# A third buffer for the conditioning slabs, single slabs at even distances, and their requests moved within ScalarE's program

## The reference, cut to what matters

```python
# first block
h = h + 0.5 * swiglu(rms_norm(h, ffn1_norm[l]), ffn1_w1[l], ffn1_w3[l], ffn1_w2[l])
...  # attention and pooling
h = h + 0.5 * swiglu(rms_norm(h, ffn2_norm[l]), ffn2_w1[l], ffn2_w3[l], ffn2_w2[l])
# second block, layers 0 and 1
cond = silu(c)
mod = cond @ ada_w[i] + ada_b[i]
sh_m, sc_m, g_m, sh_f, sc_f, g_f = split(mod, 6)
h = rms_norm(x, norm_mix[i]) * (1 + sc_m) + sh_m
```

## Time and profile before

| | us |
|---|---|
| median of 3 runs | 3036.22 |
| lowest, highest | 3034.94, 3041.8 |
| profiled execution, own time | 3037.72 |
| its span, first to last instruction | 3035.9 |
| TensorE busy | 2819.2 (93%) |
| VectorE busy | 1431.1 (47%) |
| GpSimd busy | 868.0 (29%) |
| ScalarE busy | 539.6 (18%) |

### The profile page before, as it was taken

How to read it: one execution, slowest core, us unless ns; L and a number is a source line. 1 busy time by engine, 2 the same in 40 slices (tenths; PEclk the granted TensorE clock), 3 DMA queues, 4 the chain that set the end, 5 groups by cost and what they waited for, 6 DMA issues and landing times.

```text
span 3035.9 us, 28890 instructions
## 1 busy us (share of the span) xinstructions
PE 2819.2 (93%) x11348; PEld 2009.3 (66%) x11348; DVE 1431.1 (47%) x2231; ACT 539.6 (18%) x1019; POOL 868.0 (29%) x688
## 2 busy tenths in 40 slices
PE   7998999999999998999999989999996459999999
PEld 6887885655446787885544755888543224688888
DVE  6444312156525544323279353555415992466531
ACT  2000000011201000001112251222115431222200
POOL 4444430000213433430000132443012560344432
PEclk9999999999999999999599999999997669999999
DMA  6444322211123444321011102224220001222222
GB/s 208 148 158 150 122 76 83 65 62 42 56 69 128 146 159 156 116 77 60 14 56 56 56 1 70 84 97 111 76 66 28 0 1 56 80 86 84 86 78 73
DMA packets 222626, 253.37 MB, mean 83 GB/s; under 512 B 16328, under 2 KB 209180, under 8 KB 222364
## 3 DMA queue, kind: packets, MB, share of 16 engines
q1 hardware_dynamic: 207996, 199.32, 20.8%
q10 hardware_dynamic: 14496, 52.21, 4.7%
HBM read 249.41 MB, written 2.10 MB: 83 GB/s over the span
## 4 chain that ended last, share of the span: by engine, by line
PE 79%; DVE 14%; ACT 2%; issue 2%; DMA 2%; POOL 1%; DVEq 0%; ACTq 0%; SPq 0%; POOLq 0%
PE ps L612 33%; PE ps L668 13%; PE ps L1140 9%; PE ps L498 5%; PE ps L1606 3%; PE ps L2277 3%; DVE phase L2435 2%; DMA phase<-in_ada_w 2%; PE ps L1167 1%; PE ps L1647 1%; PE ps L1659 1%; DVE phase L2420 1%; PE ps L890 1%; PE ps L1275 1%; DVE rs L1856 1%
## 5 line engine op out<-in xcount | busy, mean ns | idle before, releaser
L612 PE MATMUL ps<-hT,ring 128*128 128x256 f32 x2816 | 656.6, 381 | 2.6 <-DVE hT L954 1.0
L612 PEld LDWEIGHTS ps<-hT,ring 128*128 128x128 f32 x2816 | 538.5, 192 | 80.4 <-issue 3.5
L612 PE MATMUL ps<-phase,ring 128*128 128x256 f32 x2112 | 516.1, 389 | 53.1 <-DVE act_t L688 51.9
L612 PEld LDWEIGHTS ps<-phase,ring 128*128 128x128 f32 x2112 | 410.4, 195 | 114.8 <-DVE act_t L688 55.9
L540 POOL TENSOR_TENSOR ring<-ring 128x512 f32<-128x512 f32 (+1 forms) x124 | 160.9, 1297 | 1071.3 <-DMA ring<-in_ffn_w 582.7
L668 PE MATMUL ps<-phase,ring 128*128 128x256 f32 x1848 | 400.6, 379 | 1.0 <-issue 1.0
L668 PEld LDWEIGHTS ps<-phase,ring 128*128 128x128 f32 x1848 | 350.6, 190 | 48.8 <-issue 1.4
L1140 PE MATMUL ps<-hT,ring 128*128 128x512 f32 x512 | 228.0, 599 | 3.1 <-ACT phase L1332 2.6
L1606 PE MATMUL ps<-hT,ring 128*128 128x512 f32 x448 | 197.6, 597 | 0.6 <-ACT hT L1036 0.6
L543 POOL TENSOR_TENSOR ring<-ring 128x512 f32<-128x512 f32 (+1 forms) x124 | 188.7, 1522 | 0.0
L694 DVE TENSOR_TENSOR act_t<-u,ps 128x256 f32<-128x256 f32 x176 | 73.4, 421 | 239.1 <-PE ps L612 238.9
(11 more groups left out here) (331 smaller groups left out, 3082.5 us busy)
## 6 DMA issues: line engine op xcount, KB each, us to landing
ring<-in_ffn_w SPq DMA_DIRECT2D x60, 1024.0 KB, 5.5
phase<-in_ada_w ACTq DMA_DIRECT2D x96, 512.0 KB, 6.1
ring<-in_ffn_w_up SPq DMA_DIRECT2D x44, 1024.0 KB, 5.1
ring<-in_w_in SPq DMA_DIRECT2D x19, 1024.0 KB, 5.3
ring<-in_attn_w_in SPq DMA_DIRECT2D x14, 1024.0 KB, 5.2
ring<-in_ffn_w_down SPq DMA_DIRECT2D x8, 1408.0 KB, 6.1
ring<-in_ssm_w_glu SPq DMA_DIRECT2D x8, 1024.0 KB, 5.5
ring<-in_ffn_w_down SPq DMA_DIRECT2D x8, 1024.0 KB, 5.0
```

Of the source, the lines that this page charges most:

```text
L612: mm = pe.matmul(ps[:, 4 * w + bank_of[name], 0:HALF], left[:, c], right[name](c), start=(opens and c == 0), stop=(c == KC // 2 - 1), skip ...
```

## The change

It has five parts.

1. A third slab buffer, in `sq`. A request for slab n now waits for slab n - 3. The semaphores for landed slabs are three.
2. The table is even: one slab behind steps 3 and 5 of each `w` in every pair, 44 in all. There are no double places.
3. The other four slabs (44 to 47) stand in the first round of the down projection, in VectorE's program: ahead of the step after P6, behind the two updates that follow it, behind the step after P7, and behind the update that follows the step after P5.
4. The requests stand at other places of ScalarE's program. Three stand at the start. Then each stands behind the instruction beside which its predecessor by three is used.
5. The position tables use `acc` and `rs` in place of `sq`, and SyncE's request for the positions waits for one more event, the spread of the norm before.

The core of the diff (the exchange of tile names in the tables is left out):

```diff
-        ada_slab = [phase[:, 22528 + j * D:22528 + (j + 1) * D] for j in range(2)]
+        ada_slab = [phase[:, 22528 + j * D:22528 + (j + 1) * D] for j in range(2)] + [sq[:, :, :].rearrange("p j t -> p (j t)")]
...
                 act.activation(x[:, 0:HALF], ps[:, 0, 0:HALF], ACT.Silu).then_inc(silu_done, 1)
+                ada_load(act, k, SLAB_AT[p, 0, 3] + 3)
                 act.wait_ge(quad, quad_up(k, p, 0, 5))
...
                 if p == 0:
-                    ada_load(act, k, 0)
-                    ada_load(act, k, 1)
+                    for n in range(3):
+                        ada_load(act, k, n)
                     first(p, 1)
                 else:
-                    for n in SLAB_AT[p - 1, 1, 3]:
-                        ada_load(act, k, n + 2)
-                    for n in SLAB_AT[p - 1, 1, 5]:
-                        ada_load(act, k, n + 2)
+                    ada_load(act, k, SLAB_AT[p - 1, 1, 5] + 3)
                 silu(p)
-                for n in SLAB_AT[p, 0, 3]:
-                    if n + 2 < SLABS:
-                        ada_load(act, k, n + 2)
                 if p >= 1:
                     first(p, 1)
-                for n in SLAB_AT[p, 0, 5]:
-                    if n + 2 < SLABS:
-                        ada_load(act, k, n + 2)
+                ada_load(act, k, SLAB_AT[p, 0, 5] + 3)
                 after(p)
+                ada_load(act, k, SLAB_AT[p, 1, 3] + 3)
+            ada_load(act, k, SLAB_AT[NP - 1, 1, 5] + 3)
+            ada_load(act, k, SLAB_AT[NP - 1, 1, 5] + 4)
...
+                def slab(n):
+                    if k < 2 and q == 0:
+                        ada_slab_dve(dve, k, SLABS - 4 + n)
+
                 one, two = 2 * q + 1, 2 * q
+                slab(0)
                 dve.wait_ge(u_copied, COPIES0[k] + FC + q + 1)
                 done("P6")
...
+                slab(1)
                 done("P7")
                 dve.tensor_tensor(c22, u, ps[:, bank + 2, 0:HALF], ALU.add).then_inc(quad, 1)
+                slab(2)
                 done("P5")
...
                 quadrant(two, 1, c22).then_inc(quad, 1)
+                slab(3)
                 done("P2")
...
-            return 2 if step == 5 and w == 1 and p in (2, 4, 6, 8) else int(step == 5)
...
+        SLAB_AT = {(p, w, step): 4 * p + 2 * w + (step == 5) for p, w in UP_STEPS for step in (3, 5)}
...
-            if s >= 2:
-                act.wait_ge(ada_step, SLABS * l + s - 1)
+            if s >= 3:
+                act.wait_ge(ada_step, SLABS * l + s - 2)
...
         def positions_load(sp):
             sp.wait_ge(sum_done, 3)
+            sp.wait_ge(spread_done, 3)
```

More of the change, by code:

```diff
@@ L392, in build @@
         gated = sem("gated")
-        slab_loaded = [sem(f"slab_loaded{i}") for i in range(2)]
+        slab_loaded = [sem(f"slab_loaded{i}") for i in range(3)]
         cond_done = sem("cond_done")
@@ L764, in strassen_silu_dve @@
                         if step in (3, 5):
-                            for n in SLAB_AT[p, w, step]:
-                                ada_slab_dve(dve, k, n)
+                            ada_slab_dve(dve, k, SLAB_AT[p, w, step])
                 x, y, g = quadrants[0], quadrants[1], gT[:, 4 * p * HALF:4 * (p + 1) * HALF]
@@ L1042, in build @@
         SLABS = 6 * KC
-        def slabs_after(p, w, step):
-            if step == 3:
-                return 1
-            return 2 if step == 5 and w == 1 and p in (2, 4, 6, 8) else int(step == 5)
-        SLAB_AT, _slabs = {}, 0
-        for _p in range(NP):
-            for _w in range(2):
-                for _step in (3, 5):
-                    SLAB_AT[_p, _w, _step] = range(_slabs, _slabs + slabs_after(_p, _w, _step))
-                    _slabs += slabs_after(_p, _w, _step)
-        assert _slabs == SLABS
+        UP_STEPS = [(p, w) for p in range(NP) for w in range(2)]
+        SLAB_AT = {(p, w, step): 4 * p + 2 * w + (step == 5) for p, w in UP_STEPS for step in (3, 5)}
         SUM_AT = {}
         for _j in range(5):
-            SUM_AT[min(p for p in range(NP) if SLAB_AT[p - 1 if p else 0, 1, 5][-1] >= KC * _j + KC - 1 and p)] = _j
+            SUM_AT[min(p for p in range(1, NP) if SLAB_AT[p - 1, 1, 5] >= KC * _j + KC - 1)] = _j
         def ada_load(act, l, s):
+            if s >= SLABS:
+                return
             j, c = s // KC, s % KC
-            if s >= 2:
-                act.wait_ge(ada_step, SLABS * l + s - 1)
-            act.dma_start(ada_slab[s % 2], a["ada_w_2"][l, c * P:(c + 1) * P, j * D:(j + 1) * D])\
-                .then_inc(slab_loaded[s % 2], 16)
+            if s >= 3:
+                act.wait_ge(ada_step, SLABS * l + s - 2)
+            act.dma_start(ada_slab[s % 3], a["ada_w_2"][l, c * P:(c + 1) * P, j * D:(j + 1) * D])\
+                .then_inc(slab_loaded[s % 3], 16)
         def ada_slab_dve(dve, l, s):
             j, c = s // KC, s % KC
-            part, slab = ada_acc[j % 2], ada_slab[s % 2]
-            dve.wait_ge(slab_loaded[s % 2], 16 * (SLABS // 2 * l + s // 2 + 1))
+            part, slab = ada_acc[j % 2], ada_slab[s % 3]
+            dve.wait_ge(slab_loaded[s % 3], 16 * (SLABS // 3 * l + s // 3 + 1))
             if c == 0:
@@ L1504, in tables_dve @@
         def tables_dve(dve, p):
-            ang, k = sq[:, 0, :], sq[:, 1, :]
+            ang, k = acc[:, :], rs[:, :]
             if p >= 1:
@@ L1529, in tables_act @@
             act.wait_ge(s_ang, 8)
-            act.activation(C("sin"), sq[:, 0, :], ACT.Sin).then_inc(s_sin, 1)
-            act.activation(sq[:, 1, :], sq[:, 0, :], ACT.Abs).then_inc(s_sin, 1)
+            act.activation(C("sin"), acc[:, :], ACT.Sin).then_inc(s_sin, 1)
+            act.activation(rs[:, :], acc[:, :], ACT.Abs).then_inc(s_sin, 1)
             act.wait_ge(s_sin, 2)
-            act.activation(C("cos"), sq[:, 1, :], ACT.Sin, bias=C("half_pi"), scale=-1.0).then_inc(s_sin, 1)
+            act.activation(C("cos"), rs[:, :], ACT.Sin, bias=C("half_pi"), scale=-1.0).then_inc(s_sin, 1)
         r2 = Region()
@@ L2573, in positions_load @@
             sp.wait_ge(sum_done, 3)
-            sp.dma_start(sq[:, 1, :].bitcast(I32), a["positions_2"].to_broadcast([P, T])).then_inc(s_pos, 16)
+            sp.wait_ge(spread_done, 3)
+            sp.dma_start(rs[:, :].bitcast(I32), a["positions_2"].to_broadcast([P, T])).then_inc(s_pos, 16)
         def late_loads(act):
```

## The result

| us | before | after |
|---|---|---|
| median | 3035.72 (4 runs) | 2962.03 (4 runs) |
| lowest, highest | 3034.94, 3041.8 | 2959.73, 2962.45 |
| profiled execution, own time | 3037.72 | 2959.73 |
| its span | 3035.9 | 2957.9 |

The ratio is 0.9751, with a 95% interval of 0.9735 to 0.9768: faster, by 73.7 us between the medians, where 66 were forecast. The stated range was 2961 to 2983: the median of 2962.0 lies just inside its lower edge, and the ratio applied to the 3036.2 that the prediction started from gives 2960.6, just outside it.

The account below looks back on a forecast made before the run. TensorE, busy 93% of the span, bounds the kernel, so only its standing still or lower clock can be won. Savings of 60.3 + 6 - 0 = 66 us off 3036.2 give 2970 us, range 2961 to 2983.

Parts of the forecast that it names:

- The eight waits: Up projections, behind pairs 2, 4, 6, 8: TensorE's waits behind double slabs go, 44.15 us plus 16.1 of slow stretches, 60.3.
- my ten slow stretches: Lower TensorE clock for 8 to 9 us behind each up-projection wait: 16.1 us for eight, 1.70 and 1.58 behind pair 0.
- The double slab's request: End of pair 2: second slab's request, third in ScalarE's row until 116.9 us, leaves VectorE idle 5.93 and TensorE waiting 5.96.
- The two waits behind pair 0: Up projections: GpSimd's sums slow VectorE's chain; less overlap saves 4.5 + 2.9 = 7.4 us, taken as 6, bounds 0 to 11.0.
- How slot 4 and 5 land: Pair 0: an earlier slab request lets slot 4 land about 1.5 us earlier; the next slot likewise meets slabs spread out.
- The third buffer and the requests: Up projections: three places make 18 us, a slab needs 6.1, so VectorE's 51.3 us of waiting goes to about nothing.
- The four slabs in the down projection: Slabs ahead of the steps after P7 and P5 cost nothing, margins 1.3 and 1.4 us; at most 2 us in all.
- the rule of the Trainium skill: VectorE with two SBUF inputs contends with GpSimd reading SBUF; by it, down-projection slabs could cost 5 us in both stages.
- A: Rival: only the eight waits go, those behind pair 0 stay; 2976 us, up to 2979; chance 0.28.
- B: Rival: the waiting changes place, with half of the eight waits left at some ends of pairs; 3006 us; chance 0.07.
- C: Rival, slower: GpSimd's sums fall on every chain behind pairs 1 to 9, 4.5 us each; 3057 us; chance 0.02.
- D: Rival: no change, TensorE finds another thing to wait for at the same eight places; 3036 us; chance 0.03.

Follow-up runs that it names:

- even table: Kernel before with one slab at each place and four slabs in the down projection, two buffers, requests at old places: 2973.6 us, ratio 0.9792.
- the kernel with the buffer alone: Kernel after with the old table of double slabs, none in the down projection, and old request places, leaving only the third buffer new: 2976.5 us, ratio 0.9800.
- the experiment on the end of a pair: Kernel before with one request per pair moved from behind the next pair's first copy to its own pair's end: 2973.2 us, ratio 0.9786.
- one request moved: Kernel before with pair 0's first request (slab 2) moved ahead of the second activation part: 3030.6 us, ratio 0.9983.
- holding GpSimd back: Kernel with the even table, GpSimd's sums of slot 4 made to wait until VectorE's four sums of pair 0 are done: 2960.6 us, ratio 0.9745.
- fillers: Kernel after with extra VectorE operations behind five pairs of the first up projection: 7 to 21 of them 3002.3 us, 1 to 5 of them 2961.5.
- request back: Kernel after with pair 0's first request behind the start (slab 3) put back behind the second activation part: 2965.8 us, ratio 0.9768.
- the slabs together: Kernel after with slabs 45, 46 and 47 together ahead of the step after P7 in the down projection's first round: 2968.4 us in one run.
- the requests' places alone: Kernel before with requests at the new places only; double slabs, two buffers, none in the down projection: 2960.6 us, ratio 0.9749.

## Why the prediction was right or wrong

*The eight waits*, "sum 60.3 us": measured alone, 61.9 (even table), so right, and short by 1.6, within the noise of the medians. The traces show a shortfall too, in TensorE's busy time. It fell by 286.68 - 275.98 = 10.7 us in the first stage and by 10.9 in the second, 21.6, where my ten slow stretches summed to 19.4: about 0.2 us for each of ten restarts. It is there at the full clock as well: in the kernel with the buffer alone the product behind the 1.61 us wait took 1.83 us from its start to the next one's, where its neighbours take 1.73, and the last one ahead of the wait counts as busy to its own end, 0.16 us more.

*The double slab's request*, "third in a row of three that takes until 116.9 us": misread, without weight in the sum. ScalarE's first request behind the copy is the one for slab 12, the double's second; the third was issued at 116.5, when VectorE had slab 12 in work since 114.91. What held the request was the copy alone, 5.8 us ahead of that slab's start, and the experiment on the end of a pair shows the same.

*The two waits behind pair 0*, "I take 6": this is the step that failed, a term that was mis-sized. Kernel after against the even table alone: 2973.6 - 2962.0 = 11.6 us, against an upper bound stated as 11.0. The medians were taken on different occasions (by the two ratios it is 12.4 us, give or take some 7), but the traces bear it out: the two up projections are 4.6 and 8.8 us longer in the kernel with the table alone, and 2.3 us of that lie in their first 32 records, ahead of any of this. The first stage's part was right (all of 2.79 and its slow stretch, 4.5). In the second stage I let three sums run free and left 2.1 us of wait and the slow stretch. But the position tables' two operations stand in the same chain, and I didn't count them, though I had priced them at 2.2 us beside GpSimd for another pair. Here they are after, with step 2 of pair 1:

```profile
928.10 0.42 DVE L1505 CAST acc<-rs 128x512 f32<-128x512 int32 x1
928.55 0.48 DVE L1507 TENSOR_SCALAR acc<-acc,const 128x512 f32<-128x512 f32 x1
...
929.50 0.42 DVE L688 TENSOR_TENSOR act_t<-u,ps 128x256 f32<-128x256 f32 x1
```

And before:

```profile
968.26 1.48 DVE L1511 CAST sq<-sq 128x512 f32<-128x512 int32 x1
969.78 1.36 DVE L1513 TENSOR_SCALAR sq<-sq,const 128x512 f32<-128x512 f32 x1
...
971.61 0.42 DVE L688 TENSOR_TENSOR act_t<-u,ps 128x256 f32<-128x256 f32 x1
```

0.9 us for 2.8: these 1.9 us are most of the 2.1 that were to be left; the slab in the chain gave another 0.5 (1.38 for 1.91). With the wait its slow stretch went too. The working's own 7.4 would then have been 11; that I took 6 of 7.4 made it worse.

*How slot 4 and 5 land*, "about 1.5 us earlier, and the next slot likewise meets its two slabs spread out": slot 4's first sum started 3.1 us earlier in the execution (48.43, not 51.54). Measured from VectorE's slab, which itself started 1.4 us earlier, it was 51.56 - 48.43 = 3.1 us ahead instead of 53.00 - 51.54 = 1.5, so 1.7 us were won, about the size forecast. The second half of the sentence was the wrong way round: slot 5 must not come early too. Counted from the stage's start, GpSimd's sums of slot 4 began 2.5 and 2.9 us earlier after than before, those of slot 5 at the same time to within 0.2 us. In the second stage slot 5 itself landed some 1.5 us later than before; with one request moved it didn't, its sums stood right behind slot 4's, and 3.92 us of wait were left. Neither the sum nor a rival had named this.

*The third buffer and the requests*, "VectorE's 51.3 us of waiting goes to about nothing": right; the kernel after has no such wait. That the places, the table and the buffer are three cures for the same eight waits I had not said; I gave them to the table.

*The four slabs in the down projection*, nothing: right, 142.50 for 142.47, with the steps behind P7 and P5 here:

```profile
320.53 0.41 DVE L811 TENSOR_TENSOR u<-u,ps 128x256 f32<-128x256 f32 x1
...
322.05 0.41 DVE L817 TENSOR_TENSOR u<-u,ps 128x256 f32<-128x256 f32 x1
```

Counted in the time of the kernel before (36.5 us later at the step after P6) they start at 357.0 and 358.6, where the working had 357.2 and 358.9, and three slabs in one place gave the 1.38 us that the margins say. GpSimd was idle here from 312.5 to 330.7 us, so the rule of the Trainium skill (SBUF — State Buffer, "Who interferes with whom") had nothing to act on. Behind pair 0 the traces agree with it: a sum of VectorE of 0.42 us, with both inputs in SBUF, takes 1.37 to 1.51 beside a sum of GpSimd, and holding GpSimd back gave 0.43 again; steps 1 and 2, with one input in PSUM, kept 0.41 and 0.42 us there (62.88 and 63.42 us, before).

*Rivals.* A (only the eight) was the kernel with the table alone, 2973.6 for 2976. B, C and D didn't occur: no end behind pairs 1 to 9 has a wait.

## What to carry to other kernels

Where an engine waits for a transfer, look first at what stands ahead of the request in its issuer's program: one request per pair, moved ahead of one copy, brought 63.7 us of the 73.7. When two engines hinder each other, a late chain grows (seven fillers of some 0.45 us took 6.96), so ask where the other's next burst starts, and whether holding it back is free. When a wait is expected to go, price everything in its chain that the same cause has slowed, small operations too, and don't shade the sum afterwards.

## What was not expected of the hardware

How two queues' requests lie to each other shifts their landing by microseconds. With two slabs asked for right behind slot 4's request, GpSimd's first sum of it started 8.2 to 8.5 us behind that request (second stage, four kernels: before, the table or the buffer alone, request back); with one slab ahead and one behind, 5.6 us in the kernel after. But the latter scatters: the same stretch in the kernels with fillers and with the slabs together gave 6.1, 6.1 and 8.1. A slab's median time to landing fell from 6.1 us to 4.7 by the requests' places alone, and to about 4 with the even table as well. And TensorE's clock stayed at its upper level behind waits of up to 1.61 us, and was at the lower one behind all from 2.77 us on.
